# Two transformer blocks on one core: first loads and keys reordered, recurrence products spread over 22 turns

## The chip, the core and the metric

The kernel runs on one core of a Trainium2 chip. A core has a matrix engine (PE, TensorE), a vector engine (DVE), a scalar engine (ACT), a general engine (POOL, GpSimd) and a queue that only issues transfers (SP). Each engine works through its own list of instructions in order and waits on semaphores that other engines raise. The metric is the device time of one execution in microseconds (us), lower is better.

## What is computed

512 tokens of width 1024 pass a first block of two layers and then a second block of one layer. The change touches the first block only: its memory keys and values, its even layer's mixer, and the two MLPs beside which the second block's modulation is summed.

```
mem_n = rmsnorm(mem, mem_norm_gain)                      # 256 memory tokens
for l in range(2):
    h = rmsnorm(x, g[0])
    y = even_mixer(h, ...) if l == 0 else odd_mixer(h, ...)
    x = x + rmsnorm(y, g[1])
    h = rmsnorm(x, g[2])
    kv = mem_n @ w_kv[l]                                 # keys and values
    x = x + rmsnorm(memory_cross_attention(h, mem_n, w_q[l], w_kv[l], w_o[l]), g[3])
    h = rmsnorm(x, g[4])
    x = x + rmsnorm(squared_relu_mlp(h, w_ff1[l], w_ff2[l]), g[5])

# even_mixer: h @ w_in gives u (pooling), q, f (forget gate), i (values), g (output gate), 512 columns each
#   u: mean over 2, 4, 8 and 16 tokens less u, times a 128x128 matrix per group, times a scale
#   q, f, i, g: a gated linear recurrence with 4 heads of 128, normed per head and gated
#   both halves side by side @ w_out
mod = silu(c) @ cond_w + cond_b                          # second block's shifts, scales and gates
```

## The kernel before

**Products.** Every weight matrix comes in chunks of 1 MB into three raw buffers. SP issues the load of chunk r when chunk r - 3 is used up. A chunk has two units. For each unit ACT writes the rounded part (`act_split`, L417) and POOL the rest (`pool_split`, L425); four unit places hold them. PE multiplies three times for each tile (high by high, high by low, low by high, L439 to L441). Who splits how far ahead at which point is written out by hand: `AHEAD` is 3 units.

**Memory stage.** `pe_memory` makes for each layer eight key tiles (one unit each), then four value chunks with two token tiles each. Its first three key tiles run together (`pe_first`). ACT rounds the memory (`act_operand`), makes the root of the mean square (`act_root`, L537 and L540), and rounds x for the even layer. DVE subtracts the low parts (`dve_operand_low`, L556), scales each key tile by the root (L814, event `key_scaled`) and, between key 3 and key 4 of layer 0, makes the low parts and the sum of squares of x (L556, L563). POOL issues the constants and x at the start (L719, L721); then for each key tile c it splits unit c + 3 and issues the write of key c (L797), which waits for `key_scaled` c. Values go the same way (L802, after ACT's L787).

**Even layer.** After the products f, g and q, `pe_even` runs a loop of turns. There are 32 items, four heads by eight levels. At turn n DVE makes the decay difference of item n (L1094), ACT its exponential (L973, L975), POOL the high factor (L1233), DVE the low factor of item n - 2 (L1103), PE the pairs of item n - 4 (L891), and DVE keeps them through a mask (L1172). PE begins with turn 4. In its turns it also has one dense piece each in turns 4 to 11 (i, eight pieces) and 12 to 15 (u, four pieces). A piece stands at the head of PE's turn. The outputs of head h run in the turns of head h + 1 (L930 to L938), with the norm's sum (L520), its root on ACT, and on DVE L1207 to L1216. Pooling group g is made by DVE at turn 18 + 2g (L1146 to L1159), multiplied by PE one turn later (L879), rounded by ACT and subtracted by DVE (L1124) at turn 20 + 2g. After the loop come the outputs of head 3, then the product with w_out.

**MLP.** Up products go in groups of four tiles; group g's down product follows group g + 1's up product. Beside them DVE sums the modulation weights (`dve_mod`, L1389 and L1394) and PE adds over partitions (`pe_mod_sum`, L1415); DVE then adds the bias (`dve_mod_add`, L1407), which waits for PE's sum.

```
        I_FROM, U_FROM = 4, 12
            g = (n - 18 - delay) // 2
            return [g] if (n - delay) % 2 == 0 and 0 <= g < 4 else []
```

## Time and profile before

| | us |
|---|---|
| median of 3 runs | 4018.38 (4016.72 to 4021.52) |
| the profiled execution, its own time | 4018.33 |
| its span, first to last instruction | 4017.0 |
| PE busy | 3639.1 (91%) |
| DVE busy | 2034.4 (51%) |
| ACT busy | 1483.5 (37%) |
| POOL busy | 1529.3 (38%) |
| memory stage, loads included | 0 to 159.1 |
| even layer's f, g and q | 159.1 to 225.7 |
| the loop of turns | 225.7 to 371.8 |

The times of the stages are read from where their instructions stand in the timeline. A row of a timeline gives the start, the duration, the engine, the line, the operation and its tiles, and in brackets how long the engine had been idle before it and what ended that. A row of the windows view gives a stretch, its length, and then the busy time (and count of instructions) of PE, of PE's weight loads (PEld), of DVE, ACT and POOL; behind them stand PE's granted clock (1.00 is 2.4 GHz, 0.5 is 1.2 GHz), the share of the DMA engines in use, and GB/s.

### The profile page before, as it was taken

What the parts mean: (1) busy time and instruction counts of PE and PEld (TensorE: products, weight loads), DVE (VectorE), ACT (ScalarE), POOL (GpSimd) and SP (SyncE); (2) the same over time, 40 slices, a digit from 0 to 9 for tenths busy, and PEclk for the clock granted to TensorE, in tenths of its full rate; (3) what the DMA queues carried; (4) which work ended last, traced back from release to release, by engine and by line L of the source; (5) the groups of instructions that cost most, each with busy time, mean ns of one, the idle gap of its engine ahead of it and who ended that gap; (6) DMA issues with size and microseconds to landing.
All of it is one profiled execution on the core that took longest, in us unless ns stands there. A gap on an engine that the chain in (4) does not pass through costs nothing.

```text
span 4017.0 us, 49459 instructions
## 1 busy us (share of the span) xinstructions
PE 3639.1 (91%) x19310; PEld 2963.9 (74%) x19310; DVE 2034.4 (51%) x3613; ACT 1483.5 (37%) x2332; POOL 1529.3 (38%) x724
## 2 busy tenths in 40 slices
PE   4986889998998889988885889999999999999998
PEld 4875667887766668866774578878978888888885
DVE  2265547556345365234767418998852333323334
ACT  3553433234334342324332423336753223332222
POOL 4741324444323234433220133343344545445452
PEclk8997999999999999999995999999999999999999
DMA  4520214443212133322100123444564444444441
GB/s 158 179 78 13 82 53 139 144 137 110 84 58 74 53 116 127 103 75 76 53 3 22 35 88 114 126 132 178 212 214 138 159 143 155 149 144 156 144 157 53
DMA packets 298038, 445.36 MB, mean 111 GB/s; under 512 B 8144, under 2 KB 219088, under 8 KB 295760
## 3 DMA queue, kind: packets, MB, share of 16 engines
q1 hardware_dynamic: 278640, 371.22, 28.2%
q0 software_dynamic: 19168, 70.98, 5.5%
q8 instruction: 155, 2.54, 0.3%
q14 instruction: 75, 0.61, 0.0%
HBM read 383.45 MB, written 58.72 MB: 110 GB/s over the span
## 4 chain that ended last, share of the span: by engine, by line
PE 74%; DVE 17%; ACT 4%; issue 3%; POOL 1%; DMA 1%; DVEq 0%; POOLq 0%; ACTq 0%; SPq 0%
PE bank L439 21%; PE bank L441 20%; PE bank L440 20%; PE bank L2586 3%; PE bank L520 2%; DVE arena_rw L2111 2%; POOL split_low L425 1%; PE bank L1630 1%; DVE arena L2675 1%; PE bank L1654 1%; DVE arena L2769 1%; DVE arena L2677 1%; DVE arena L2681 1%; PE bank L1288 1%; PE bank L1915 1%
## 5 line engine op out<-in xcount | busy, mean ns | idle before, releaser
L425 POOL TENSOR_TENSOR split_low<-weights,split_high 128x1024 fp32r<-128x1024 f32 x554 | 1387.6, 2511 | 2128.9 <-ACT split_high L417 2128.1
L439 PE MATMUL bank<-normed_high,split_high 128*128 128x512 f32 x2480 | 988.5, 399 | 76.0 <-issue 38.8
L440 PE MATMUL bank<-normed_low,split_high 128*128 128x512 f32 x2480 | 974.6, 393 | 0.0
L441 PE MATMUL bank<-normed_high,split_low 128*128 128x512 f32 x2480 | 973.7, 393 | 0.0
L417 ACT CAST split_high<-weights 128x1024 fp32r<-128x1024 f32 x554 | 574.6, 1048 | 676.1 <-PE bank L441 572.2
L439 PEld LDWEIGHTS bank<-normed_high,split_high 128*128 128x128 f32 x2480 | 471.8, 190 | 185.9 <-issue 52.3
L439 PE MATMUL bank<-hidden_high,split_high 128*128 128x512 f32 x1536 | 600.9, 391 | 7.0 <-ACT hidden_high L2670 4.8
L441 PE MATMUL bank<-hidden_high,split_low 128*128 128x512 f32 x1536 | 599.2, 390 | 0.0
L440 PE MATMUL bank<-hidden_low,split_high 128*128 128x512 f32 x1536 | 599.0, 390 | 0.0
L440 PEld LDWEIGHTS bank<-normed_low,split_high 128*128 128x128 f32 x2480 | 472.2, 190 | 99.1 <-issue 3.1
L441 PEld LDWEIGHTS bank<-normed_high,split_low 128*128 128x128 f32 x2480 | 471.1, 190 | 100.2
L1438 DVE TENSOR_TENSOR branch<-branch,bank 128x512 f32<-128x512 f32 x360 | 243.0, 686 | 510.4 <-PE bank L441 510.2
L439 PEld LDWEIGHTS bank<-hidden_high,split_high 128*128 128x128 f32 x1536 | 289.2, 188 | 68.6 <-ACT hidden_high L2670 5.9
L441 PEld LDWEIGHTS bank<-hidden_high,split_low 128*128 128x128 f32 x1536 | 289.1, 188 | 60.5
L440 PEld LDWEIGHTS bank<-hidden_low,split_high 128*128 128x128 f32 x1536 | 289.3, 188 | 59.8
L2717 DVE TENSOR_TENSOR tmp<-tmp,gates 128x512 f32<-128x512 f32 x56 | 42.4, 757 | 273.1 <-ACT tmp L2657 245.4
L1394 DVE SCALAR_TENSOR_TENSOR tmp<-weights,scalars,tmp 128x256 f32<-128x256 f32 x168 | 155.9, 928 | 5.1
L1491 ACT ACTIVATE arena<-arena 128x512 f32<-128x512 f32 x64 | 40.4, 632 | 263.1 <-DVE arena L1512 263.1
L1512 DVE SCALAR_TENSOR_TENSOR arena<-bank,tmp 128x512 f32<-128x512 f32 x64 | 43.8, 689 | 179.8 <-PE bank L441 171.1
L2527 ACT ACTIVATE branch<-bank 128x512 f32<-128x512 f32 x72 | 43.1, 598 | 239.8 <-PE bank L441 239.8
L2586 PEld LDWEIGHTS bank<-arena 128*128 128x128 f32 x1024 | 120.7, 195 | 7.0 <-issue 5.2
L2586 PE MATMUL bank<-arena 128*128 128x128 f32 x1024 | 121.3, 278 | 4.5 <-DVE arena L2698 3.7
(387 smaller groups left out, 4475.5 us busy)
## 6 DMA issues: line engine op xcount, KB each, us to landing
weights<-in_w_ff SPq DMA_DIRECT2D x64, 1024.0 KB, 5.4
weights<-in_peer_u SPq DMA_DIRECT2D x64, 1024.0 KB, 5.8
weights<-in_peer_v SPq DMA_DIRECT2D x64, 1024.0 KB, 5.1
gate_table<-arena SPq DMA_DIRECT2D x16, 2048.0 KB, 7.4
gates<-gate_table POOLq DMA_DIRECT2D x32, 1024.0 KB, 9.8
weights<-in_cond_w SPq DMA_DIRECT2D x24, 1024.0 KB, 5.2
early_table<-branch SPq DMA_DIRECT2D x72, 256.0 KB, 2.1
lates<-early_table POOLq DMA_DIRECT2D x18, 1024.0 KB, 11.0
```

The lines of the kernel that those rows point to most:

```text
L417: act.do.copy(unit_tiles(u)[0], raw_unit(u)).then_inc(*act.sig("split_high", u))
L425: pool.do.tensor_tensor(lo, raw_unit(u), hi.bitcast(F32), ALU.subtract).then_inc(*pool.sig("split_low", u))
L439: pe.do.matmul(o, ah, bh, start=first, stop=False)
L440: pe.do.matmul(o, ah, bl, start=False, stop=False)
L441: return pe.do.matmul(o, al, bh, start=False, stop=last)
L520: pe.do.matmul(banks.tile("sum", norm)[:, 0:n], matrix, rhs, start=i == 0, stop=i == count - 1).then_inc(*pe.sig("summed", norm, i))
L1394: dve.do.scalar_tensor_tensor(out=total, in0=wt[:, a, :], scalar=g_act[:, CT + a:CT + a + 1], in1=total, op0=ALU.mult, op1=ALU.add).then_i ...
L1438: dve.do.tensor_tensor(y[:, c, :], y[:, c, :], made, ALU.add).then_inc(*dve.sig("y_sum", st, n, c))
L1512: dve.do.scalar_tensor_tensor(out=s, in0=banks.tile("product", (st, "up", g), c), scalar=0.0, in1=root, op0=ALU.max, op1=ALU.mult).then_in ...
L2111: dve.do.scalar_tensor_tensor(out=conv[:, c, :], in0=src, scalar=wc, in1=conv[:, c, :], op0=ALU.mult, op1=ALU.add).then_inc(*dve.sig("conv ...
L2527: act.do.activation(s, banks.tile("product", ("early", g), c), ACT.Gelu).then_inc(*act.sig("gelu", g, c))
L2586: last = pe.do.matmul(bank[:, j * P:(j + 1) * P], hot[:, 0, t, :], hot[:, 1, t, :], start=True, stop=True)
```

## The change

The change does five things.

- **First loads.** POOL issues the load of x only when the memory and the first two key chunks (chunk 0 and 1) have landed. ACT no longer splits four units first: it splits two, then interleaves the next two with the rounding of the memory.
- **Keys.** ACT splits one unit (4) instead of three before the root, and interleaves the rounding of x with the units of the keys. POOL issues the write of key c three splits later (`KEY_LAG`), and the writes of the values likewise. DVE works on x after key 7 instead of after key 3.
- **Modulation sums.** In the second up group of each MLP PE's first three sums stand one product later than before (the first and second) or where they stood (the third).
- **Recurrence.** The second i chunk is loaded and used after u. The pieces stand at turns 4, 6, 8, 10 (i, first chunk), 11, 13, 15, 17 (u), 19, 21, 23, 25 (i, second chunk). Pooling group g is at turn 14 + 2g.
- **Rounding of the mixer's result.** The pooled tiles are first kept in the place of u (`pooled_kept`), since the i products still read the operand. ACT rounds them at turns 29 to 32, the heads 0, 1, 2 at turns 27, 28, 35, and DVE subtracts one turn later. ACT has four instructions more.

```diff
-        for n in "fgqiu":
-            W["E", n] = stream(dram["w_in_ab"], n0="uqfig".index(n) * 512, n_cols=512)
+        W["E", "i"] = []
+        for n, first, n_cols in (("f", 0, 512), ("g", 0, 512), ("q", 0, 512), ("i", 0, 256), ("u", 0, 512), ("i", 256, 256)):
+            ids = stream(dram["w_in_ab"], n0="uqfig".index(n) * 512 + first, n_cols=n_cols)
+            W["E", n] = W["E", "i"] + ids if n == "i" else ids
...
+            pool.wait_ge(at("constants_landed", constant_names[-1]), at("memory_landed"), landed("chunk", 1))
             pool.do.dma_start(x, dram["x"].rearrange("(c p) t -> p c t", p=P)).then_inc(*pool.land("x_landed"))
-            pool.wait_ge(at("constants_landed", constant_names[-1]))
...
-            act_split(AHEAD)
+            first = 2 * W["keys", 0][0]
             for c in range(CT):
+                act_split(first + min(1 + c // 2, FIRST))
                 act_operand("mem", c, mem_raw[:, c, :], mem_gain, mem_hi[:, c, :], mem_square[:, c, :],
                             at("memory_landed"))
-            act_split(2 * W["keys", 0][0] + FIRST + AHEAD)
+            act_split(first + FIRST + 1)
             act_root("mem", 0, NORM_EPS, mem_root, M)
-            for c in range(CT):
-                act_operand(EM, c, x[:, c, :], gain_of(0, 0), h_hi[:, c, :], y[:, c, :], at("x_landed"))
             for l in range(2):
                 for c in range(CT):
                     act_split(2 * W["keys", l][0] + c + AHEAD)
+                    if l == 0:
+                        act_operand(EM, c, x[:, c, :], gain_of(0, 0), h_hi[:, c, :], y[:, c, :], at("x_landed"))
...
                     pool_split(2 * W["keys", l][0] + c + AHEAD)
-                    pool.wait_ge(at("key_scaled", l, c))
-                    pool.do.dma_start(memory_k[l, c], k_out.tile(l, c)).then_inc(*pool.land(*k_written(l, c)))
-                for n, i in enumerate(W["values", l]):
-                    for tk in range(M // P):
-                        pool_split(2 * i + tk + AHEAD - 1)
-                        pool.wait_ge(at("value_scaled", l, n, tk))
-                        pool.do.dma_start(memory_v[l, tk][:, n * 256:(n + 1) * 256], v_out.tile(l, n, tk)
-                                          ).then_inc(*pool.land(*v_written(l, n, tk)))
+                    if c >= KEY_LAG:
+                        pool_key_out(l, c - KEY_LAG)
+                tokens = [(n, tk) for n in range(len(W["values", l])) for tk in range(M // P)]
+                for m, (n, tk) in enumerate(tokens):
+                    pool_split(2 * W["values", l][n] + tk + AHEAD - 1)
+                    if m < KEY_LAG:
+                        pool_key_out(l, CT - KEY_LAG + m)
+                    else:
+                        pool_value_out(l, *tokens[m - KEY_LAG])
+                for n, tk in tokens[-KEY_LAG:]:
+                    pool_value_out(l, n, tk)
+
+        KEY_LAG = 3
+
+        def pool_key_out(l, c):
+            pool.wait_ge(at("key_scaled", l, c))
+            pool.do.dma_start(memory_k[l, c], k_out.tile(l, c)).then_inc(*pool.land(*k_written(l, c)))
+
+        def pool_value_out(l, n, tk):
+            pool.wait_ge(at("value_scaled", l, n, tk))
+            pool.do.dma_start(memory_v[l, tk][:, n * 256:(n + 1) * 256], v_out.tile(l, n, tk)
+                              ).then_inc(*pool.land(*v_written(l, n, tk)))
...
-                    if l == 0 and c == 3:
-                        dve_token_root("mem", 2, 4)
-                        for e in range(CT):
-                            dve_operand_low(EM, e, x[:, e, :], gain_of(0, 0), h_hi[:, e, :], h_lo[:, e, :],
-                                            at("x_landed"))
-                        dve_operand_sum(EM, lambda e: y[:, e, :])
+                if l == 0:
+                    dve_token_root("mem", 2, 4)
+                    for e in range(CT):
+                        dve_operand_low(EM, e, x[:, e, :], gain_of(0, 0), h_hi[:, e, :], h_lo[:, e, :], at("x_landed"))
+                    dve_operand_sum(EM, lambda e: y[:, e, :])
...
-        I_FROM, U_FROM = 4, 12
+        I_TURNS, U_TURNS = (4, 6, 8, 10, 19, 21, 23, 25), (11, 13, 15, 17)
+        PIECE_TURNS = sorted(I_TURNS + U_TURNS)
+
+        UNIT_PIECE = (3, 3, 4, 5, 6, 7, 11, 11)
+        HEAD_FINALS, POOL_FINALS = {27: 0, 28: 1, 35: 2}, {29: 0, 30: 1, 31: 2, 32: 3}
 
         def pool_at(n, delay):
 
-            g = (n - 18 - delay) // 2
+            g = (n - 14 - delay) // 2
             return [g] if (n - delay) % 2 == 0 and 0 <= g < 4 else []
 
         def rec_units(n):
 
-            if n < I_FROM:
-                return 2 * W["E", "i"][0] + AHEAD - 1
-            if n < U_FROM:
-                return 2 * W["E", "i"][(n - I_FROM) // TT] + AHEAD - ((n - I_FROM) % TT == 0)
-            return 2 * W["E", "u"][0] + min(n - U_FROM, 4) + AHEAD
-
+            return 2 * W["E", "i"][0] + 3 - (n < 5) + sum(PIECE_TURNS[j] < n for j in UNIT_PIECE)
...
-                next(i_product if n < U_FROM else u_product, None)
+                if n in PIECE_TURNS:
+                    next(i_product if n in I_TURNS else u_product)
...
-                    banks.give(("pooled", g), ("mixed_low", EM, g))
+                    banks.give(("pooled", g), ("pooled_kept", g))
...
-            pe.wait_ge(empty, at("pairs_kept", hd, N_LV - 1), at("rec_v", 1, 3))
+            pe.wait_ge(empty, at("pairs_kept", hd, N_LV - 1), at("rec_v", hd // 2, 3))
...
-                if I_FROM <= n < U_FROM:
-                    i, tk = (n - I_FROM) // TT, (n - I_FROM) % TT
+                if n in I_TURNS:
+                    i, tk = I_TURNS.index(n) // TT, I_TURNS.index(n) % TT
...
-                    act.wait_ge(at("pooled", g), at("product", (EM, "u"), 3))
-                    act.do.activation(h_hi[:, g, :], banks.tile("pooled", g), ACT.Identity, scale=col("pool_scale", g)
-                                      ).then_inc(*act.sig("mixed_high", EM, g))
+                    act.wait_ge(at("pooled", g))
+                    act.do.activation(upad[:, g, POOL_PAD:], banks.tile("pooled", g), ACT.Identity,
+                                      scale=col("pool_scale", g)).then_inc(*act.sig("pooled_kept", g))
+                if n in HEAD_FINALS:
+                    act_rec_final(HEAD_FINALS[n])
+                if n in POOL_FINALS:
+                    g = POOL_FINALS[n]
+                    act.wait_ge(at("pooled_kept", g), at("product", (EM, "i"), 1, 3))
+                    act.do.copy(h_hi[:, g, :], upad[:, g, POOL_PAD:]).then_inc(*act.sig("mixed_high", EM, g))
...
-            yield
-            act.wait_ge(at("rec_gated", hd), at("product", (EM, "u"), 3))
-            act.do.copy(h_hi[:, 4 + hd, :], s).then_inc(*act.sig("mixed_high", EM, 4 + hd))
+
+        def act_rec_final(hd):
+            act.wait_ge(at("rec_gated", hd), at("product", (EM, "i"), 1, 3))
+            act.do.copy(h_hi[:, 4 + hd, :], e_q[:, hd, :]).then_inc(*act.sig("mixed_high", EM, 4 + hd))
...
-                if 0 <= n - U_FROM < 4:
-                    dve_scaled((EM, "u"), [n - U_FROM], lambda c: upad[:, c, POOL_PAD:])
+                if n in U_TURNS:
+                    dve_scaled((EM, "u"), [U_TURNS.index(n)], lambda c: upad[:, c, POOL_PAD:])
                 for g in pool_at(n, 0):
                     dve_pooling(g)
-                for g in pool_at(n, 2):
+                if n - 1 in HEAD_FINALS:
+                    dve_rec_final(HEAD_FINALS[n - 1])
+                if n - 1 in POOL_FINALS:
+                    g = POOL_FINALS[n - 1]
                     dve.wait_ge(at("mixed_high", EM, g))
-                    dve.do.scalar_tensor_tensor(out=h_lo[:, g, :], in0=banks.tile("pooled", g),
-                                                scalar=col("pool_scale", g), in1=h_hi[:, g, :].bitcast(F32),
-                                                op0=ALU.mult, op1=ALU.subtract).then_inc(*dve.sig("mixed_low", EM, g))
+                    dve.do.tensor_tensor(h_lo[:, g, :], upad[:, g, POOL_PAD:], h_hi[:, g, :].bitcast(F32), ALU.subtract
+                                         ).then_inc(*dve.sig("mixed_low", EM, g))
+            dve_rec_final(2)
             run(dve_rec_output(REC_HEADS - 1))
+            dve_rec_final(REC_HEADS - 1)
...
+        def dve_rec_final(hd):
             dve.wait_ge(at("mixed_high", EM, 4 + hd))
-            dve.do.tensor_tensor(h_lo[:, 4 + hd, :], s, h_hi[:, 4 + hd, :].bitcast(F32), ALU.subtract
+            dve.do.tensor_tensor(h_lo[:, 4 + hd, :], e_q[:, hd, :], h_hi[:, 4 + hd, :].bitcast(F32), ALU.subtract
                                  ).then_inc(*dve.sig("mixed_low", EM, 4 + hd))
...
-                        if g == 1 and c == 0:
-                            mod_sums(0, 1)
-                            mod_sums(0, 3)
-                        mod_sums(g, c)
+                        if g == 1 and c < GROUP - 1:
+                            if c:
+                                mod_sums(c - 1, 5 - 2 * c)
+                        else:
+                            mod_sums(g, c)
```

On POOL, at the start of the key tiles of layer 0 (`memory_k` is the write of a key tile). Before:

```order
13 L425 TENSOR_TENSOR split_low<-weights_78,split_high 128x1024 x2
14 L425 TENSOR_TENSOR split_low<-weights_79,split_high 128x1024 x2
15 L797 DMA memory_k<-arena 128x256
16 L425 TENSOR_TENSOR split_low<-weights_80,split_high 128x1024
17 L797 DMA memory_k<-arena 128x256
18 L425 TENSOR_TENSOR split_low<-weights_80,split_high 128x1024
```

After:

```order
13 L427 TENSOR_TENSOR split_low<-weights_78,split_high 128x1024 x2
14 L427 TENSOR_TENSOR split_low<-weights_79,split_high 128x1024 x2
15 L427 TENSOR_TENSOR split_low<-weights_80,split_high 128x1024 x2
16 L427 TENSOR_TENSOR split_low<-weights_78,split_high 128x1024
17 L816 DMA memory_k<-arena 128x256
18 L427 TENSOR_TENSOR split_low<-weights_78,split_high 128x1024
```

The first write of a key stood behind four splits and stands behind seven.

On DVE, in the memory stage (L814 before and L832 after scale the keys, L556 and L563, then L558 and L565, work on x). Before:

```order
4 L814 TENSOR_TENSOR arena<-bank,arena 128x256 x4
5 L581 COPY token_root<-bank 128x2
6 L556 SCALAR_TENSOR_TENSOR normed_low<-residual,columns,normed_high 128x512 x8
7 L563 TENSOR_TENSOR branch<-branch 128x512 x7
8 L814 TENSOR_TENSOR arena<-bank,arena 128x256 x12
```

After:

```order
4 L832 TENSOR_TENSOR arena<-bank,arena 128x256 x8
5 L583 COPY token_root<-bank 128x2
6 L558 SCALAR_TENSOR_TENSOR normed_low<-residual,columns,normed_high 128x512 x8
7 L565 TENSOR_TENSOR branch<-branch 128x512 x7
8 L832 TENSOR_TENSOR arena<-bank,arena 128x256 x8
```

The 15 instructions on x moved behind four more keys.

On PE, in the loop, at the first pooled product (L879 before, L897 after; L891 and L909 are pairs, L439 to L441 and L441 to L443 a dense piece, here of u). Before:

```order
1372 L891 MATMUL bank<-branch 128x128 x8
1373 L520 MATMUL bank<-tmp_60,arena 128x512
1374 L891 MATMUL bank<-branch 128x128 x4
1375 L879 MATMUL bank<-tmp_62,branch 128x512
1376 L891 MATMUL bank<-branch 128x128 x4
1377 L891 MATMUL bank<-arena 128x128 x4
```

After:

```order
1245 L441 MATMUL bank<-normed_high,split_high 128x512
1246 L442 MATMUL bank<-normed_low,split_high 128x512
1247 L443 MATMUL bank<-normed_high,split_low 128x512
1248 L897 MATMUL bank<-tmp_62,branch 128x512
1249 L909 MATMUL bank<-branch 128x128 x4
1250 L948 MATMUL bank<-arena 128x128
1251 L951 MATMUL bank<-arena 128x128
```

A dense piece now stands ahead of the pooled product, where only pairs stood.

## Rows read from the trace of the kernel before

**Rows 1.** Windows, memory stage and loop: stretch, length, then busy us by engine

```profile
39.37:45.81 6.44, 0.00 (x1) 0.03 (x1) 1.42 (x4) 6.40 (x12) 3.08 (x3) 0.88 0.06 20
60.19:77.65 17.46, 0.00 (x1) 0.03 (x1) 11.55 (x20) 0.00 (x0) 5.90 (x5) 0.63 0.05 16
77.65:159.07 81.42, 73.04 (x579) 71.59 (x579) 3.40 (x8) 29.63 (x39) 69.49 (x49) 0.97 0.59 196
225.73:286.40 60.67, 59.08 (x415) 55.06 (x414) 39.96 (x55) 33.49 (x52) 32.15 (x22) 1.00 0.22 70
286.40:371.80 85.40, 44.69 (x226) 36.67 (x225) 60.77 (x114) 38.51 (x59) 14.82 (x16) 0.76 0.04 13
```

**Rows 2.** Timeline of POOL in the memory stage

```profile
4.64 0.90 POOL L721 DMA_DIRECT2D residual<-in_x  x1
16.55 9.48 POOL L425 TENSOR_TENSOR split_low<-weights,split_high 128x1024 fp32r<-128x1024 f32 x4 [11.00 <-ACT split_high L417]
42.70 0.58 POOL L797 DMA_DIRECT2D memory_k<-arena  x1 [16.67 <-DVE arena L814]
...
71.71 0.56 POOL L797 DMA_DIRECT2D memory_k<-arena  x1 [17.30 <-DVE arena L814]
...
98.50 2.37 POOL L425 TENSOR_TENSOR split_low<-weights,split_high 128x1024 fp32r<-128x1024 f32 x1 [0.17 <-ACT split_high L417]
```

**Rows 3.** Timeline of ACT in the memory stage

```profile
11.46 0.21 ACT L1378 ACTIVATE scalars<-columns 128x8 f32<-128x8 f32 x1
15.35 1.99 ACT L417 CAST split_high<-weights 128x1024 fp32r<-128x1024 f32 x2 [3.68 <-DMA weights<-in_w_mem_kv]
...
41.46 0.42 ACT L540 ACTIVATE arena<-arena 128x256 f32<-128x256 f32 x1
...
50.84 1.99 ACT L417 CAST split_high<-weights 128x1024 fp32r<-128x1024 f32 x2
```

**Rows 4.** DMA queues from 10 to 15 us: packets, MB, share of 16 engines

```profile
q0 software_dynamic: 370, 1.52, 81.1%
q1 hardware_dynamic: 387, 0.38, 23.5%
```

**Rows 5.** Timeline of DVE: x in the memory stage, then a modulation step in MLP 0

```profile
60.31 5.39 DVE L556 SCALAR_TENSOR_TENSOR normed_low<-residual,columns,normed_high 128x512 fp32r<-128x512 f32 x8
...
625.82 2.51 DVE L1394 SCALAR_TENSOR_TENSOR tmp<-weights,scalars,tmp 128x256 f32<-128x256 f32 x1
628.25 0.15 DVE L1407 SCALAR_TENSOR_TENSOR modulation<-bank,columns 128x2 f32<-128x2 f32 x1
```

**Rows 6.** Windows of single turns: one with an i piece, one with u, two bare

```profile
242.12:245.89 3.77, 3.77 (x35) 3.77 (x33) 2.73 (x4) 3.05 (x5) 2.75 (x4) 1.00 0.76 241
270.36:277.42 7.06, 7.06 (x40) 6.07 (x39) 5.09 (x6) 2.74 (x5) 3.55 (x2) 1.00 0.10 31
286.20:288.15 1.95, 1.95 (x18) 1.76 (x16) 1.95 (x3) 0.00 (x0) 1.95 (x3) 1.00 0.00 0
```

**Rows 7.** Waits in loop and tail (225.73 to 394.41): total, times, longest

```profile
DVE arena L1172 <- PE bank L891: 29.2, 15, 4.0
...
PE bank L879 <- DVE tmp L1159: 23.1, 4, 6.6
```

**Rows 8.** Groups by line in the loop: count, busy us, mean ns, idle before

```profile
L1094 DVE TENSOR_TENSOR branch<-arena 128x512 f32<-128x512 f32 x28 | 24.3, 876 | 0.0
L1172 DVE COPY_PREDICATED arena<-arena,bank 128x512 f32<-128x512 uint32 x28 | 20.5, 732 | 29.2 <-PE bank L891 29.2
...
L1147 DVE TENSOR_TENSOR arena<-arena 128x527 f32<-128x527 f32 (+3 forms) x10 | 7.0, 697 | 0.0
```

**Rows 9.** Timeline of PE in MLP 0, second up group

```profile
618.87 0.98 PE L1415 MATMUL bank<-const_mean,tmp 128*128 128x1 f32 x4 [5.23 <-DVE tmp L1394]
...
621.52 0.77 PE L439 MATMUL bank<-normed_high,split_high 128*128 128x512 f32 x1 [1.67 <-POOL split_low L425]
```

**Rows 10.** Timeline of ACT at the same place

```profile
617.91 1.04 ACT L417 CAST split_high<-weights 128x1024 fp32r<-128x1024 f32 x1
```

3 lines of the change are left out of this document (2 added, 1 removed).

## The prediction

> **What bounds the kernel now.** I read the windows by stage first, to see where PE idles, then the timelines of POOL, ACT and DVE in those stretches, to see who comes last. The change touches three places.
>
> *Memory stage.* PE does nothing for 6.44 us from 39.37 and for 17.46 us from 60.19 [rows 1]. Both times POOL is the one it lacks, and POOL in turn waited 16.67 and 17.30 us at the write of a key for DVE's scaling of that key [rows 2]: first because the root ends at 41.88 [rows 3], then because DVE works on x from 60.31 [rows 5], 11.55 us busy in the stretch [rows 1]. Splits that PE needs are queued behind these two writes on POOL. From 77.65 on PE is busy 73.04 of 81.42 us [rows 1]: there the split is held by ACT's half of it (0.17 us of wait on ACT at 98.50 [rows 2]), which follows ACT's scaling of a value tile.
>
> *Loop of turns.* Up to 286.4 PE is busy 59.08 of 60.67 us; afterwards 44.69 of 85.40, while DVE is busy 60.77 and the granted clock is 0.76 [rows 1]. All dense pieces lie in the first part. In the second, PE waits 23.1 us for DVE's pooling before four products and DVE waits for pairs, 29.2 us over the loop [rows 7]. Each waits for the other, in turn.
>
> *MLP.* PE waits 5.23 us for the modulation sum and then 1.67 us for a split [rows 9].
>
> The rest of the kernel is not touched.
>
> **First loads.** Between 10 and 15 us the queue with x moved 1.52 MB and the one with the keys 0.38 MB [rows 4]; chunk 0 landed at about 15.3 [rows 3]. So at 10 us some 0.4 MB of it were missing; at the 0.38 MB per us of both queues together it lands at about 11.1 and chunk 1 at 13.9. But POOL waits for chunk 1 before it issues x (0.90 us [rows 2]), and its splits are queued behind that: they start at 14.8 instead of 16.55. ACT, free at 11.67 [rows 3], is in time. The gain is 1.8 us where chunk 0 alone would give 3.7. PE's three first tiles go on from the third split, so from about 22.1 instead of 24.0. A few of its products have run before that, so I put the root, now done at 41.88 [rows 3], at 39.6. Bounds: 0 to 4 us earlier.
>
> **Keys and x.** Split 4 follows the first three tiles directly (ACT 34.2, POOL 36.6 by 2.37 us each [rows 2]), so key 4 starts as the sum ends, and the 6.44 us are gone. What is late next is split 5: ACT does the root and two of the eight x steps first (8.96 us for eight from 41.88 to 50.84 [rows 3], 2.2 for two), so 41.8, split 42.9, POOL 45.3. PE idles about 5.3 us there. Then POOL paces: splits of 2.37 with a write of 0.58 [rows 2] give 47.7, 50.6, 53.6 and 56.5 for units 6 to 9, and the values of layer 0 start at 56.5 instead of 77.65: 21.1 us. DVE's 11 us on x now run beside the values, and x is wanted at the end of the stage: nothing.
>
> Small terms behind that. The first value product ran partly at the low clock (0.97 in the stretch [rows 1], so up to 2.4 us of 81.42): minus 1.8. `token_root` is now copied after key 7, whose buffer waits for the write of key 3, three splits back: one value split is late by 0.9. Value tile m needs the buffer of m - 4, whose write is issued one step later than its own split: 0 to 2 us, I take 1. The sum of the stage is 21.1 + 1.8 - 0.9 - 1 - 0.5 = **20.5 us** gained, bounds 13 and 25.
>
> DVE on x and POOL now run at the same time, which the trace has elsewhere: an instruction of DVE with two SBUF inputs took 2.51 us at 625.82 where a split ran [rows 5]. The Trainium skill ("SBUF — State Buffer", section "SBUF: two separate sides") says that such a DVE instruction and a GpSimd one that reads SBUF lock each other out for a whole instruction, whichever starts first. By it the 15 instructions could hold up eight splits by up to 0.7 us each, 5 us on this path instead of the 0.5 above; with DVE off the path it costs nothing there.
>
> **The loop.** The cost of a turn on PE: 3.77 us with an i piece, 7.06 with u (outputs in it), 0.97 bare [rows 6]. On DVE the decay difference takes 0.88 and the masked copy 0.73 [rows 8]; with the low factor (0.6, my estimate between these and its half width) that is 2.2 per turn, waits for POOL's port included. A step of pooling is 0.70 [rows 8], so group g takes about 0.7 (g + 1) + 1.8. I walk the new turns in four parts.
> - Turns 4 to 10: PE 4 x 3.77 + 3 x 0.97 = 18.0. DVE has 7 x 2.2 = 15.4, head 0's keys 2.5 and 5 of backlog: 23. DVE bounds.
> - Turns 11 to 18: PE 4 x 7.06 + 4 x 0.97 + 2 pooled products of 1 = 34. DVE 17.6, keys and outputs 6, pooling 0 and 1 5.7: 29. PE bounds, and its u pieces cover pooling 0 and 1, which in the old order covered nothing: that is where the wait of 23.1 [rows 7] shrinks.
> - Turns 19 to 27: DVE 9 x 2.2 + keys and outputs 7 + pooling 2 and 3 8.5 less overlap = 33; an i piece of 2.8 doesn't cover 3.9 and 4.6, so DVE also waits twice for a pooled product and pairs (2 each) and once for a root: 38.
> - Turns 28 to 35: the same work as before, some 21 from turn 28's start to its last pair, plus six roundings moved here (0.6 each), less two waits of 0.7 for ACT: 24.
>
> Together 119, with 2 for stretches at the low clock 121, against 145 now. The loop gains **24 us**. Its bounds: DVE was busy 39.96 + 60.77 = 100.7 us in it [rows 1], so no more than 45; and 0, if every turn waits as in the second part now. Kept for the range: 8 and 36. ACT's four extra copies (0.6 each) lie beside DVE in turns 28 to 32. The splits of the second i chunk and of w_out come one to eight turns before their use. The tail after the loop (outputs of head 3, first tiles of w_out) stays, since it hangs on head 3.
>
> **Modulation sums.** I cost this edit at a small loss. The sum's wait of 5.23 us [rows 9] covers another one: the next product needs a split whose ACT half began at 617.91 [rows 10], after DVE's chain, with no link to the sum. PE would wait until 621.52 anyway. The sum (0.5 us at full clock) leaves an idle stretch for a busy one, and DVE's bias step at 628.25 [rows 5] now waits for it about 0.9 us, with the next `relu` queued behind it. **Plus 1 us** for both MLPs; bounds 0 and 3.
>
> **Sum.** 4018.33 (the profiled execution; the median of the runs, 4018.38, is the same) - 20.5 - 24 + 1 = 3974.8, so 3975.
>
> **Rivals.**
> 1. *PE stays at the low clock in turns 19 to 35.* It has 34 us of work there at full clock (4 x 2.8 + 17 x 0.97 + 6) with waits between. At 0.76 it was busy 44.69 in the second part now [rows 1]. If half of the turns run at the low level, 16 us come back, and the loop gains 8: 3991. Against it: the u pieces now fill the middle. Chance 0.15. The Trainium skill ("TensorE: Matmul & The Clock Gate", section "HAM oscillation — how this bites in real kernels") says that a PE that waits between bursts falls back to half rate again and again; by that rule, this case.
> 2. *The loop reaches DVE's own time,* 101 to 105 us, since waits vanish with balance: 3956. For it: DVE had idle time only where it waited for PE. Against: pooling still stands between two pairs. Chance 0.1.
> 3. *The modulation sums bring their wait,* 5.2 us in each MLP, because the split comes sooner than I read: 3964. Against: [rows 9, 10]. Chance 0.06.
> 4. *Port.* The memory stage gains 13 because splits and DVE lock each other out: 3982. Chance 0.1.
> 5. *Slower.* A piece at the head of a turn holds the pairs back, DVE waits for them, and the next turn's output waits for DVE, so that PE and DVE never overlap. Then the loop takes PE's 84 us (32 x 0.97 + 8 x 2.8 + 4 x 5.7 + 8) plus DVE's 100.7 = 185 instead of 146: 4018 - 20 + 39 + 1 = 4038. It decides from a loop of 166 us on. Against it: up to 286.4 PE was busy 59.08 and DVE 39.96 us of 60.67 [rows 1], which is overlap. Chance 0.04.
> 6. *The change doesn't do what it says:* x's load or the key writes turn out to wait longer than they did (chunk 1 late, a full ring of four key buffers), and both gains stay under 4 us: about 4012. Chance 0.02.
>
> **Numbers.** The forecast has 0.53. Its own bounds are 4018 - 25 - 36 + 0 = 3957 and 4018 - 13 - 8 + 3 = 4000, which takes in rivals 1, 3, 4 and nearly 2. A measurement of this kernel tells 0.2%, 8 us, from no change. Faster 0.94, same 0.02, slower 0.04.
>
> **What would show it.** Memory stage: POOL's first split at 14.8; one idle of about 5 us before key 5; values from about 56; the stage's end (first f product) near 138.5. Loop: some 120 us long, PE's wait before the pooled products under 12 us, DVE over 80% busy in it. MLP: the wait before the second product of the group grows to about 7.9 us and ends on the split. Wrong would be a wait on a key write that reappears, a loop over 137 us, or a wait at the sum's new place.

## The result and the profile after

The changed kernel takes 3989.55 us (median of 4 runs, 3986.77 to 3990.26) against 4017.72 us for the kernel before (4 runs, 4016.72 to 4021.52): the ratio is 0.993, with a 95% interval of 0.9918 to 0.9942. It is faster, by 28.2 us; 43.5 us were forecast. Profiled execution against profiled execution, the gain is 4018.33 - 3986.77 = 31.6 us. By the places where PE starts its stages, 18.7 us of it come before the first f product (now at 140.41, 159.07 before), 12.4 us in the loop up to the first product of `w_out` (133.64 us long instead of 146.08), and 0.5 us in the two MLP groups. f, g and q between them take 66.66 us in both.

The windows of the changed kernel, which answer to [rows 1] (stretch, length, then busy us and instructions of PE, PEld, DVE, ACT and POOL, the granted clock, DMA share, GB/s): the gap before key 5, the values of layer 0, from there to the first f product, and the loop in two parts.

```profile
38.91:44.06 5.15, 0.01 (x1) 0.03 (x1) 0.90 (x3) 5.15 (x8) 2.50 (x2) 0.95 0.00 0
55.18:87.98 32.80, 26.44 (x192) 25.92 (x193) 19.45 (x18) 9.77 (x14) 22.59 (x17) 0.90 0.49 165
87.98:140.41 52.43, 47.67 (x389) 46.56 (x387) 3.40 (x8) 19.77 (x25) 46.67 (x33) 1.00 0.61 201
207.07:268.47 61.40, 55.88 (x348) 48.98 (x347) 47.83 (x75) 33.26 (x52) 28.03 (x21) 0.97 0.16 52
268.47:340.71 72.24, 45.75 (x293) 40.12 (x292) 54.95 (x93) 40.29 (x64) 21.57 (x16) 0.83 0.09 30
```

The two idle stretches of [rows 1], 6.44 and 17.46 us, have become one of 5.15. But the values of layer 0, PE from 77.65 to 106.85 in the kernel before, now take longer:

```profile
77.65:106.85 29.20, 25.61 (x193) 25.09 (x193) 0.00 (x0) 9.86 (x14) 22.43 (x17) 0.93 0.56 185
```

The same work takes 32.80 instead of 29.20 us. Why, the timelines of the changed kernel tell: DVE (scaling of the keys 4 to 7, then the root of the tokens), then ACT (scaling of value tiles), each with the idle time ahead of it and what ended it.

```profile
38.39 1.42 DVE L832 TENSOR_TENSOR arena<-bank,arena 128x256 f32<-128x256 f32 x4 [7.37 <-ACT arena L542]
49.65 0.42 DVE L832 TENSOR_TENSOR arena<-bank,arena 128x256 f32<-128x256 f32 x1 [9.84 <-DMA memory_k<-arena]
...
59.91 0.42 DVE L832 TENSOR_TENSOR arena<-bank,arena 128x256 f32<-128x256 f32 x1 [4.27 <-DMA memory_k<-arena]
60.25 0.15 DVE L583 COPY token_root<-bank 128x2 f32<-128x2 f32 x1
60.32 9.72 DVE L558 SCALAR_TENSOR_TENSOR normed_low<-residual,columns,normed_high 128x512 fp32r<-128x512 f32 x8
```

```profile
60.49 0.48 ACT L790 ACTIVATE arena<-bank,token_root 128x256 f32<-128x256 f32 x1 [6.88 <-DVE token_root L583]
...
78.17 0.47 ACT L790 ACTIVATE arena<-bank,token_root 128x256 f32<-128x256 f32 x1 [3.33 <-DMA memory_v<-arena]
```

Keys go through four buffers. Key 7 needs the one of key 3, whose write POOL now issues three splits after its turn and which has to land; so it is scaled at 59.91, the root of the tokens is copied behind it, and ACT, which scales the values by it, stands idle for 6.88 us with the next split queued behind. PE waits 3.57 us for that split and then starts at the low level (granted clock 0.90 in the stretch). Some of these 6.88 us ACT would have waited anyway, for PE's first product of values (run `lag1` below tells how many). Value tiles meet the same ring: 15.6 us of waits of ACT on `memory_v`, six of them.

The waits in the loop and the tail (207.07 to 363.2), total, times, longest, against [rows 7]:

```profile
DVE arena L1202 <- PE bank L909: 21.9, 12, 4.7
...
PE bank L897 <- DVE tmp L1189: 12.4, 2, 7.0
```

DVE's waits for pairs went from 29.2 to 21.9 us, PE's for the pooled product from 23.1 (four times) to 12.4 (twice). The two left are groups 2 and 3. PE, DVE and POOL at group 2:

```profile
278.43 2.08 PE L897 MATMUL bank<-tmp,branch 128*128 128x512 f32 x2 [7.04 <-DVE tmp L1189]
280.29 1.92 PE L909 MATMUL bank<-branch 128*128 128x128 f32 x8
```

```profile
272.70 2.34 DVE L1176 COPY arena<-arena 128x2 f32<-128x2 f32 x1
...
278.89 0.42 DVE L1129 TENSOR_TENSOR branch<-arena,branch 128x256 f32<-128x256 f32 x1
282.25 0.73 DVE L1202 COPY_PREDICATED arena<-arena,bank 128x512 f32<-128x512 uint32 x1 [2.94 <-PE bank L909]
```

```profile
272.68 2.34 POOL L427 TENSOR_TENSOR split_low<-weights,split_high 128x1024 fp32r<-128x1024 f32 x1 [5.77 <-ACT split_high L419]
...
314.18 5.24 POOL L427 TENSOR_TENSOR split_low<-weights,split_high 128x1024 fp32r<-128x1024 f32 x2 [6.12 <-ACT split_high L419]
```

Two things stand here. PE waits 7.04 us for the mean of the group with the pair of the same turn queued behind it, and DVE then waits 2.94 us for that pair. And DVE's copy of two columns takes 2.34 us, exactly as long as POOL's split beside it; its like took 0.17. The same happens in part at DVE's turn 28 (the splits stand in POOL's turn 26), where the second of these POOL rows covers two splits:

```profile
314.98 2.23 DVE L1120 TENSOR_TENSOR branch<-arena 128x512 f32<-128x512 f32 x1
317.13 2.57 DVE L1129 TENSOR_TENSOR branch<-arena,branch 128x256 f32<-128x256 f32 x1
```

Their like took 0.68 and 0.42.

In MLP 0 PE's wait is now in one piece, and the sum comes behind the second product ([rows 9] has 5.23 and 1.67):

```profile
590.23 0.77 PE L441 MATMUL bank<-normed_high,split_high 128*128 128x512 f32 x1 [7.87 <-POOL split_low L427]
...
597.12 0.50 PE L1447 MATMUL bank<-const_mean,tmp 128*128 128x1 f32 x4
```

A word on the measure. In all twelve kernels below, the part behind the loop, from the first product of `w_out` to the last of PE, is nearly the same code, and in the profiled executions it took between 3627 and 3636 us. At one place in it, a group of eight products took 3.67 us in the changed kernel (from 461.07, granted clock 1.00 around it) and 5.37 in `lag1` (from 458.82, granted clock 0.84). So single times carry some 5 us that say nothing of an edit, and small effects are read below from where PE's stages start.

### The profile page after: what moved, and what is told of

It reads as the page before. It is cut to its first block, busy times and chain, and to the rows that moved or that the text cites. A ratio compares the mean times of both kernels' runs of the same rounds, so it can differ in the third digit from the quotient of the medians.

```text
span 3985.5 us, 49467 instructions
## 1 busy us (share of the span) xinstructions
PE 3638.2 (91%) x19310; PEld 2962.6 (74%) x19310; DVE 2050.4 (51%) x3613; ACT 1484.3 (37%) x2336; POOL 1529.6 (38%) x724
## 4 chain that ended last, share of the span: by engine, by line
PE 73%; DVE 16%; ACT 4%; issue 3%; POOL 2%; DMA 1%; DVEq 0%; POOLq 0%; ACTq 0%; SPq 0%
PE bank L441 21%; PE bank L443 20%; PE bank L442 20%; PE bank L2619 3%; PE bank L522 2%; DVE arena_rw L2144 2%; POOL split_low L427 2%; DVE arena L2708 1%; PE bank L1663 1%; DVE arena L2802 1%; DVE arena L2710 1%; DVE arena L2714 1%; PE bank L1687 1%; PE bank L1320 1%; PE bank L1948 1%
## 5 line engine op out<-in xcount | busy, mean ns | idle before, releaser
L441 PE MATMUL bank<-normed_high,split_high 128*128 128x512 f32 x2480 | 991.3, 400 | 88.5 <-issue 38.8
L443 PE MATMUL bank<-normed_high,split_low 128*128 128x512 f32 x2480 | 976.1, 394 | 0.0
L441 PEld LDWEIGHTS bank<-normed_high,split_high 128*128 128x128 f32 x2480 | 473.3, 191 | 200.0 <-issue 65.9
L441 PE MATMUL bank<-hidden_high,split_high 128*128 128x512 f32 x1536 | 601.0, 391 | 6.9 <-ACT hidden_high L2703 4.7
L443 PE MATMUL bank<-hidden_high,split_low 128*128 128x512 f32 x1536 | 599.2, 390 | 0.0
L443 PEld LDWEIGHTS bank<-normed_high,split_low 128*128 128x128 f32 x2480 | 472.2, 190 | 100.7
L441 PEld LDWEIGHTS bank<-hidden_high,split_high 128*128 128x128 f32 x1536 | 289.2, 188 | 68.5 <-ACT hidden_high L2703 5.8
L443 PEld LDWEIGHTS bank<-hidden_high,split_low 128*128 128x128 f32 x1536 | 289.2, 188 | 60.5
L2750 DVE TENSOR_TENSOR tmp<-tmp,gates 128x512 f32<-128x512 f32 x56 | 42.4, 756 | 272.9 <-ACT tmp L2690 245.5
```

The lines of the kernel that those rows point to most:

```text
L441: pe.do.matmul(o, ah, bh, start=first, stop=False)
L443: return pe.do.matmul(o, al, bh, start=False, stop=last)
```

## The experiments

**Each part alone.** `mem_only` is the kernel before with the memory stage of the change and nothing else; `loop_only` has the new chunk order and the new loop alone.

```
mem_only:  pool_inputs, act_memory, pool_memory (KEY_LAG 3), dve_memory of the change
loop_only: SHARED, W["E"], I_TURNS, U_TURNS, UNIT_PIECE, pool_at, the finals of the change
```

> The kernel before with the memory stage alone changed (x issued behind chunk 1, splits and key writes in the new order, x behind the keys of layer 0); loop and modulation sums as before. Account A (additive: each part of the change gives what its stage gave in the changed kernel, where the first f product starts 18.7 us earlier): the stage brings 18.7 us, so about 4018.4 - 18.7 = 3999.7, within 2. Rival B (the memory stage's gain is partly paid back in the loop by transfers or splits that meet it earlier, and the loop's shortfall is that debt): the stage again starts f 18.7 us earlier, but the time falls by 10 us or less, 4008 and more.

> The kernel before with the recurrence loop alone changed (chunk order f, g, q, i1, u, i2, pieces over 22 turns, pooling two to four turns earlier, roundings behind it). Account A (additive; the loop is short of its 24 us by its own waits and has nothing to do with the memory stage): 12 us, so about 4006. The forecast's own number for this part was 24 us, 3994. Rival B (interaction with the memory stage): the loop alone brings 20 us or more, 3998 or less.

`mem_only` took 4004.17 us (4000.52 to 4013.33) against 4017.11 for the kernel before on the same chip, ratio 0.9974, interval 0.9961 to 0.9986. `loop_only` took 4005.25 (4001.59 to 4015.95), ratio 0.9977, 0.9966 to 0.9989. Here are the windows of the two loops, `mem_only` first:

```profile
206.51:352.25 145.74, 104.31 (x639) 92.03 (x638) 99.61 (x168) 72.07 (x111) 47.96 (x37) 0.84 0.11 37
```

```profile
226.04:358.42 132.38, 101.24 (x640) 89.41 (x638) 102.09 (x168) 73.49 (x115) 49.97 (x37) 0.88 0.12 40
```

In `mem_only` f starts at 139.85, 19.2 us earlier than in the kernel before, and its loop is as long as before. In `loop_only` the loop is 13.7 us shorter. Together that is 32.9 us, where the change has 18.7 + 12.4 = 31.1: the parts add, and the loop's shortfall is no debt of the memory stage. By the medians they are 12.9 and 11.9 us, 24.8 together where the change has 28.2. `loop_only` is where its account A had it (4006); the median of `mem_only` is 4.5 us above what was expected. The part behind its loop was 1.8 us longer than before in the profiled execution; for the other executions nothing shows where it went.

**Modulation sums back in their old place,** in the changed kernel:

```
-                        if g == 1 and c < GROUP - 1:
-                            if c:
-                                mod_sums(c - 1, 5 - 2 * c)
-                        else:
-                            mod_sums(g, c)
+                        if g == 1 and c == 0:
+                            mod_sums(0, 1)
+                            mod_sums(0, 3)
+                        mod_sums(g, c)
```

> The changed kernel with the modulation sums back in their old place. Account A (the sum's wait only covered the wait for the split): the same time as the changed kernel within 2 us, 3987 to 3992, and in the trace the second up product starts as long behind the first one as in the kernel before. Rival C (moving the sums brought their waits of 5.2 us each, and the loop gained less): 10 us slower than the changed kernel, 3999.

3988.60 us (3980.52 to 3993.18), ratio 0.9924, interval 0.9908 to 0.9941. The wait is in two pieces again, and the second up product starts at 589.94, 7.89 us behind the first one's end; in the changed kernel it is 7.87.

```profile
587.28 0.98 PE L1447 MATMUL bank<-const_mean,tmp 128*128 128x1 f32 x4 [5.24 <-DVE tmp L1426]
589.94 0.77 PE L441 MATMUL bank<-normed_high,split_high 128*128 128x512 f32 x1 [1.67 <-POOL split_low L427]
```

From the end of the first up product to the down products of the group before it is 27.91 and 28.24 us in the changed kernel (MLP 0 and 1), 28.97 and 29.00 with the sums in their old place. That is 1.8 us less in all with the sums moved. But the kernel before, with the same old order, took 27.31 and 29.37 us, 1.3 us less in all than `sums_undone`, so most of the 1.8 can be chance. In the time nothing is seen, and the wait of 5.2 us was never to be had.

**Writes one split behind instead of three.**

```
-        KEY_LAG = 3
+        KEY_LAG = 1
```

> The changed kernel with the writes of keys and values one split behind instead of three (KEY_LAG 1). Account A (in the changed kernel the writes come so late that the ring of four buffers is full: DVE waits up to 4.3 us for a key's write to land, so the root of the tokens comes at 60.3, and ACT waits 2.2 to 3.3 us for value writes; the value stage of layer 0 takes 32.8 us instead of 29.2): the waits on landed writes go, values of layer 0 take 29 us, f starts 3.5 to 4.5 us earlier, 3985 to 3986. Rival D (the value stage is longer because DVE's work on x and POOL's splits share a port): the splits stay as long and late, no gain, 3989.5. Rival E (with the writes earlier POOL waits for the scaling of keys again, as before the change): values of layer 0 start 2 us or more later than 55.2, and the kernel is slower than 3990.

3988.90 us (3980.61 to 3991.63), ratio 0.993, interval 0.9914 to 0.9947: by the time alone this cannot be told from the changed kernel. By the trace it can. Windows of the values of layer 0 and of the rest up to f, then DVE's last key and ACT's first value:

```profile
55.80:84.01 28.21, 23.78 (x193) 23.26 (x193) 25.10 (x15) 9.87 (x14) 23.47 (x17) 1.00 0.58 192
84.01:136.18 52.17, 47.44 (x388) 46.50 (x387) 3.40 (x8) 19.77 (x25) 46.77 (x33) 1.00 0.61 202
```

```profile
54.39 0.42 DVE L832 TENSOR_TENSOR arena<-bank,arena 128x256 f32<-128x256 f32 x1 [2.45 <-PE bank L443]
54.73 0.15 DVE L583 COPY token_root<-bank 128x2 f32<-128x2 f32 x1
```

```profile
58.95 0.47 ACT L790 ACTIVATE arena<-bank,token_root 128x256 f32<-128x256 f32 x1 [5.25 <-PE bank L443]
```

From key 5 on no wait on a write is left (key 4 still waits 1.37 us for one); keys and values wait for PE's products alone. ACT's first value waits for PE until 58.95, 3.2 us after the values start; in the changed kernel it came 5.3 us after that, so the late token root cost ACT some 2 us. The values take 28.21 us instead of 32.80, at full clock, and f starts at 136.18, 4.2 us earlier. Rival D falls with it: DVE's 15 steps on x take even longer beside the splits (26.8 us, 19.3 in the changed kernel, 10.85 in the kernel before), and hold up little. PE's three waits for splits within the values are 4.4 us, 3.6 in the kernel before, where no DVE step stood beside them: 0.8 us. Rival E falls too, since the values start at 55.80.

**ACT's half of split 5 ahead of the root.**

```
-            act_split(first + FIRST + 1)
+            act_split(first + FIRST + 2)
             act_root("mem", 0, NORM_EPS, mem_root, M)
```

> The changed kernel with ACT's half of split 5 ahead of the root of the memory instead of behind it and two x steps. In the changed kernel it began at 40.46 and PE stood 5.15 us ahead of key 5. Account A (PE waits for the split alone, and POOL paces the keys from then on): ACT's half at 33.2, POOL's at 38.0, the wait before key 5 goes, the root comes up to 0.5 us later; values of layer 0 start at 51 to 52 instead of 55.2, f 3 to 4 us earlier. Rival F (writes: a key's scaling needs a free buffer and the writes are issued by POOL behind these splits): keys 4 to 7 are scaled as late as now, token root at 60 as now, so ACT waits for it still and f starts within 1 us of 140.4.

One run, 3989.58. The wait before key 5 is gone, but PE waits 3.40 us before key 6: ACT now does three x steps at once before the next split, at 42.54.

```profile
42.02 0.62 ACT L554 ACTIVATE branch<-residual 128x512 f32<-128x512 f32 x1
42.54 1.03 ACT L419 CAST split_high<-weights 128x1024 fp32r<-128x1024 f32 x1
```

The values start at 54.89 instead of the 51 to 52 of account A, and f at 139.49, 0.9 us earlier: the outcome of rival F. The write ring (the token root came at 59.3, the waits on `memory_k` stayed) is a part of it, and the wait that moved one key on is the other, which neither account had.

**The pair ahead of the pooled product.** In PE's turn, the pooled product goes behind the pair and the output:

```
-                for g in pool_at(n, 1):
-                    ...
                 bank, empty = banks.take("pairs", hd, lv)
                 ...
                 next(outputs, None)
                 next(turns, None)
+                for g in pool_at(n, 1):
+                    ...
```

> The changed kernel with PE's pooled product queued behind the pair (and the output) of its turn instead of ahead of them. In the changed kernel PE waits 7.04 and 5.39 us for the means of groups 2 and 3 with the next pair queued behind, and DVE then waits 2.94 and 2.93 us for that pair (1.19 and 1.17 at groups 0 and 1). Account L (the loop is short of its gain because DVE and PE take turns at the pooled products): DVE's waits for these pairs go, the loop takes 128 us instead of 133.6. Rival C (it is the low clock in turns 19 to 35: the same matmuls at half the rate): PE's waits move elsewhere, the loop stays within 2 us of 133.6. Rival P (the port between DVE and the splits that the change moved into turns where DVE sets the pace): also within 2 us.

One run, 3982.15. The loop takes 130.23 us. DVE's waits for pairs fall from 21.9 to 16.4, the 5.5 us that were expected; but DVE is 3.2 us longer busy (105.99 instead of 102.77), and the loop gets 3.4. The same loop in `best1` (below) takes 126.66. So the edit is worth 3.4 to 7 us, against the 5.6 of account L (128); here is the second part of the loop in the two kernels:

```profile
267.89:336.72 68.83, 49.11 (x302) 43.60 (x300) 57.26 (x93) 39.86 (x63) 19.09 (x16) 0.80 0.09 31
```

```profile
262.69:327.95 65.26, 45.01 (x299) 40.83 (x299) 55.77 (x93) 39.77 (x63) 21.84 (x16) 0.84 0.10 33
```

The 3.6 us between them come in three pieces. 1.2 us come before the pooled product of group 3, where the pair at the start of this part took PE 1.91 us at the low level in `pair_first`, so that DVE kept it 1.4 us later. 0.8 us come at the last root, whose product took 2.07 us in `pair_first` and 1.13 in `best1`. The other 1.6 us (9.58 against 7.99 us from one output's product to the root's) lie between, where POOL's last three multiplications stand beside DVE's steps. In the changed kernel, as in `best1`, POOL's are long and DVE's as long as ever:

```profile
325.52 2.53 POOL L1265 TENSOR_TENSOR branch<-arena,branch 128x256 f32<-128x256 f32 x1 [3.76 <-ACT branch L993]
328.53 1.93 POOL L1265 TENSOR_TENSOR branch<-arena,branch 128x256 f32<-128x256 f32 x1 [0.48 <-ACT branch L993]
```

In `pair_first` POOL's are short, and DVE's three steps beside them take 1.22, 1.21 and 0.94 us, 0.5 each more than their like:

```profile
319.41 0.99 POOL L1265 TENSOR_TENSOR branch<-arena,branch 128x256 f32<-128x256 f32 x1 [3.76 <-ACT branch L993]
322.95 0.99 POOL L1265 TENSOR_TENSOR branch<-arena,branch 128x256 f32<-128x256 f32 x1 [2.55 <-ACT branch L993]
```

`split5` and `warm` fell as `pair_first` did, the other kernels with the new loop (`loop_only`, `sums_undone`, `lag1`, `thin`, `pair_thin`, `pair_thin_warm`, `best1`, `best2`) as the changed kernel. These are the times that two engines would show that shut each other out of a port, POOL waiting in the one case and DVE in the other. The code of that place is the same, and nothing here shows what decides it. With these 1.6 us taken off, the pair's edit is worth 5.0 us.

**Three thin splits.** POOL splits one eighth of units 9, 10 and 11 of the loop (those at 272.7 and 314.2); the other seven eighths of the low part of these weights are left out:

```
+                few = slice(0, 1 if u - 2 * W["E", "i"][0] in (9, 10, 11) else chunks[u // 2].n_k)
-                pool.do.tensor_tensor(lo, raw_unit(u), hi.bitcast(F32), ALU.subtract
+                pool.do.tensor_tensor(lo[:, few], raw_unit(u)[:, few], hi.bitcast(F32)[:, few], ALU.subtract
```

> The changed kernel in which POOL splits only 128 of 1024 columns of three units of weights: those whose splits ran at 272.7 and 314.2 to 319.4, where DVE sets the pace (most of the low half of these weights is left out of the computation; ACT's halves and all products stay). Rival P (port: DVE's instructions beside these splits took 2.2 + 0.5 and 1.6 + 2.2 + 1.0 us longer than their like): the excess goes, the loop takes 127 to 129 us instead of 133.6. Account L (turn taking at the pooled products) and rival C (clock): DVE's time there is covered by waits anyway, the loop takes 132 to 134.

One run, 3991.50. The loop takes 130.38 us, 3.3 less, and DVE's busy time in it falls from 102.77 to 96.66, all of it in the second part:

```profile
269.46:338.44 68.98, 49.56 (x293) 44.45 (x292) 48.87 (x93) 40.17 (x64) 15.93 (x16) 0.80 0.10 31
```

The port is real and was worth 6.1 us of DVE; a little over half of that reaches the loop's length, because DVE waits 2.8 us more: 1.7 for ACT's exponentials of a head (L1207 here), 0.5 for pairs, 0.6 for an output. The expectation of rival P was 127 to 129 us, that of the others 132 to 134; the measured 130.4 lies between. Both edits together:

> Both loop edits together: the pooled product behind the pair, and three POOL splits cut to 128 of 1024 columns (most of the low half of these weights left out). Alone they made the loop 130.2 and 130.4 us long instead of 133.6. If turn taking and port are two causes that add: 133.6 - 3.4 - 3.3 = 127, within 1. If both only free the same wait: 130. If together they release more than alone, since either cause hid the other: 124 or less.

One run, 3980.72. The loop takes 123.41 us, 10.2 less than in the changed kernel, and 121 had been forecast for it:

```profile
267.64:329.65 62.01, 46.53 (x302) 41.22 (x301) 49.16 (x93) 40.30 (x64) 16.64 (x16) 0.88 0.10 34
```

Against 127 for simple addition and 124 for causes that cover each other, this is the second. But with the pair's edit at 5.0 us simple addition gives 125.3, and the 1.9 us that remain are no more than the low level moved this loop between `pair_first` and `best1` (1.2 + 0.8). That the causes cover each other is not shown.

**Is it the clock?** Idle products of 128x512 fill PE's waits ahead of two pooled products (12 each, then 18) and of two heads' outputs (8 each, then 12), in banks that the true product overwrites; first in the changed kernel, then on top of both edits. The lines for the pooled products:

```
+                    for _ in range(12 if g >= 2 else 0):
+                        pe.do.matmul(bank, h_hi[:, 0, 0:P], h_hi[:, 0, :], start=True, stop=True)
                     pe.wait_ge(at("pool_mean", g), at("pool_w_landed"))
```

> The changed kernel with 12 idle products of 128x512 on PE ahead of the pooled products 2 and 3, and 8 ahead of the outputs of heads 2 and 3, in banks that the true product then overwrites: PE is busy where it waited. Rival C (clock): the products and pairs behind the waits run at full clock (1.1 + 1.1 us instead of 2.1 + 1.9), DVE's waits of 2.9 us shrink by 1.8 each, the loop takes 127 to 130 us instead of 133.6. Account L: the waits are for DVE and not for PE's rate, the loop stays within 1.5 us of 133.6; more than 135 if the idle products themselves come to stand in the way.

> The kernel with both loop edits, and on top 18 idle products of 128x512 ahead of pooled products 2 and 3 and 12 ahead of the outputs of heads 2 and 3, so that PE is busy in its waits. With the causes of turn taking and port taken away, what the low clock is worth by itself: rival C (clock) says that the granted clock of the last 72 us, 0.84, goes to 0.95 or more and the loop loses another 4 to 6 us, some 122. The account without the clock says that it stays within 1.5 us of the kernel with both edits, about 127, whatever the granted clock is.

One run each, 3991.94 and 3975.73. The loops take 133.61 and 122.58 us. The second part in both:

```profile
267.50:339.71 72.21, 54.09 (x334) 47.15 (x332) 56.65 (x93) 40.30 (x64) 18.79 (x16) 0.88 0.09 30
```

```profile
268.47:329.65 61.18, 53.49 (x359) 47.56 (x359) 49.31 (x93) 39.79 (x63) 16.20 (x16) 0.97 0.11 35
```

In `warm` the length stayed, but not because the clock did nothing. In the second part it rose from 0.83 to 0.88. At group 2 the idle products ended 4.35 us before the mean, and the product behind was still at the low level, 2.08 us. At group 3 they ended 1.99 us before it, and there the product took 1.12 us and the pair 1.05; in the changed kernel they took 2.07 and 1.91. Here is that product, `warm` first:

```profile
291.13 1.12 PE L900 MATMUL bank<-tmp,branch 128*128 128x512 f32 x2 [1.99 <-DVE tmp L1195]
```

```profile
292.06 2.07 PE L897 MATMUL bank<-tmp,branch 128*128 128x512 f32 x2 [5.39 <-DVE tmp L1189]
```

From that pair to the last three multiplications of POOL the loop of `warm` is 1.9 us ahead of the changed kernel's. There it falls the other way, DVE's steps take 1.22, 1.21 and 0.95 us, and 1.6 us are lost again. So account L came out by its number, in part by luck. In `pair_thin_warm`, where these multiplications go as in `pair_thin`, the clock is 0.97 instead of 0.88 and the second part 0.8 us shorter. The low level of these turns follows from PE's waits. It costs 0.8 us where both edits are in, 1.9 at group 3 of the changed kernel, and at its group 2, where the idle products came too early, it was not tested. That is well under the 8 us of rival 1, which came out near the measured time by the wrong road.

**A version from the findings.** `best1` is the changed kernel with KEY_LAG 1, split 5 ahead of the root, splits of the keys two ahead of the x steps, and the pair ahead of the pooled product. `best2` mends what its trace showed:

```
best1:  KEY_LAG = 1;  act_split(2 * W["keys", l][0] + c + AHEAD + (2 if l == 0 else 0))
best2:  KEY_LAG = 2;  act_split(2 * W["keys", l][0] + (min(c + AHEAD + 2, 11) if l == 0 else c + AHEAD))
        UNIT_PIECE = (3, 3, 4, 5, 6, 7, 11), unit 11 by ACT at turn 33; and behind POOL's loop:
+            pool.wait_ge(at("mixed_low", EM, 3))
+            pool_split(rec_units(N_TURNS))
```

> The changed kernel with the edits that the runs so far point to: writes one split behind (KEY_LAG 1), ACT's half of split 5 ahead of the root, ACT's splits of the keys two further ahead of its x steps, and the pooled product behind the pair. Expected: the wait before key 5 gone and no new one over 1.5 us before key 6, values of layer 0 from 50 instead of 55.2 and 28.2 us long instead of 32.8, f from 130 to 131.5 instead of 140.4, loop 130.2 instead of 133.6, modulation as in the changed kernel: 13 us faster than the changed kernel, 3975 to 3978. If POOL paces the keys whatever ACT does (a split of 2.4 and a write of 0.58 each from 38.9 on), values start at 52 or later and 3 us of this are missing.

`best1`: 3980.49 us (3977.43 to 3985.62), ratio 0.9909, interval 0.9892 to 0.9926. f starts at 134.63 instead of the 130 to 131.5 that were expected. The time is 2.5 us above the 3975 to 3978 that were expected. With one split of lag, the write of key 0 stands ahead of split 5, and POOL waits there for DVE's scaling of that key, which follows the root (from 38.51; the row below names PE as the releaser, the code waits for DVE); PE still idles 3.31 us before key 5:

```profile
39.23 0.57 POOL L816 DMA_DIRECT2D memory_k<-arena  x1 [3.48 <-PE bank L443]
39.82 2.37 POOL L427 TENSOR_TENSOR split_low<-weights,split_high 128x1024 fp32r<-128x1024 f32 x1
```

> The kernel best1 with three repairs: writes two splits behind (KEY_LAG 2) so that POOL does split 5 before it waits for key 0; ACT's splits run ahead of its x steps only up to unit 11, so that none waits 5.15 us for PE in front of the value scaling; and the last split of the loop (unit 11) taken by POOL after DVE's last rounding, when DVE waits for the last pairs, instead of at turn 27. Expected if these three waits were what best1 lacked: the 3.31 us before key 5 go, values of layer 0 from 50 instead of 54, f at 130 to 131 instead of 134.6; DVE's step of 2.57 us beside that split back to 0.4, the loop 1 to 3 us shorter than in best1 and in the kernel with the pair ahead alone (126.7 and 130.2: 124 to 128); in all 3973 to 3976. If DVE's later writes take up the port time wherever they stand, the loop stays at 127 to 130 and the time at 3977 to 3980. If the later split holds up the fourth tile of w_out in the tail, the loss shows there: more than 3.6 us of wait ahead of it.

`best2`: **3967.43 us** (3966.41 to 3970.86), ratio 0.9873, interval 0.9857 to 0.9889: 50.6 us faster than the kernel before on the same chip and 22 under the changed kernel's median. POOL does splits 4 and 5 in one go and then writes; f starts at 132.25, 8.2 us earlier than in the changed kernel (the values at 52.19, not 50: PE waits 1.19 us at key 6 and 2.35 at the first value). The loop takes 125.15 us, 8.5 less. The two stages give 16.7 us together, and profiled execution against profiled execution the gain is 15.9; so of the 22 us between the medians some 5 are not explained, nor is it shown why the time is below the 3973 to 3976 that were expected. DVE still waits 10.7 us for the landings of key writes (four times, 4.2 at most), but the token root comes at 52.64, before ACT needs it. The split moved behind POOL's loop lies in DVE's wait for the last pairs:

```profile
33.70 4.76 POOL L427 TENSOR_TENSOR split_low<-weights,split_high 128x1024 fp32r<-128x1024 f32 x2 [8.58 <-ACT split_high L419]
39.59 0.57 POOL L816 DMA_DIRECT2D memory_k<-arena  x1 [1.13 <-PE bank L443]
...
318.15 2.34 POOL L427 TENSOR_TENSOR split_low<-weights,split_high 128x1024 fp32r<-128x1024 f32 x1 [2.85 <-DVE normed_low L1153]
```

```profile
300.07 2.24 DVE L1120 TENSOR_TENSOR branch<-arena 128x512 f32<-128x512 f32 x1
302.23 1.07 DVE L1129 TENSOR_TENSOR branch<-arena,branch 128x256 f32<-128x256 f32 x1
...
320.41 0.73 DVE L1202 COPY_PREDICATED arena<-arena,bank 128x512 f32<-128x512 uint32 x1 [2.34 <-PE bank L903]
```

DVE's step that took 2.57 us beside the second split takes 1.07 (POOL's next multiplication is still beside it), and the wait ahead of the fourth tile of `w_out` is 3.61 us, as in the changed kernel.

## Why the prediction was right in its direction and too large by half

Faster was right, and the time lies in the range (3957 to 4000), 15 us above the forecast. Of the three terms, one held, one fell short by 2 us and one by half.

*First loads: near in sum.* Chunk 1 landed at 14.37 (13.9 in the estimate), but POOL's first split began at 15.95 instead of 14.8, a gain of 0.6 us and not 1.8. The root ended at 38.29, 1.3 us earlier than put, by a road that was not in the sum: with the rounding of the memory between ACT's splits, DVE's low parts begin at 14.15 instead of 22.14, and PE, whose first product waited for them until 24.01, begins at 18.46. The sum is near by two errors that go opposite ways, which is luck.

*Keys and x: right to the value stage.* The idle stretch before key 5 is 5.15 us (5.3 forecast), it ends on the split, and the values start at 55.18 (56.5). That is 22.5 us gained where 21.1 were summed.

*Small terms: the step that failed in this stage.* The sum took 2.4 us for the late token root, the ring of value buffers and the port, and gave 1.8 for the clock, 0.6 net. The stage of values lost 3.6 us, of which `lag1` gives back more than all (28.21 us). The prediction had both mechanisms, the buffer that waits for the write of three splits back and the value buffer of m - 4, and priced them by the issue of the write alone. What was left out is its landing: in the changed kernel the writes took a median of 3.7 us (keys) and 4.1 (values) from issue to landing, and that of key 3, issued at 54.96, released DVE at 59.91.

```profile
memory_k<-arena POOLq DMA_DIRECT2D x8, 128.0 KB, 3.7
memory_v<-arena POOLq DMA_DIRECT2D x8, 128.0 KB, 4.1
```

So the token root came at 60.25, 5.5 us later than in `lag1` (54.73), and ACT's first value some 2 us late, not 0.9. PE waited 3.57 us for the split behind it where it waits 1.44 in `lag1`, and the products that follow took 8.66 us at the low level instead of 5.98. These 2.1 and 2.7 us make up the difference between the two kernels' values (32.80 and 28.21), and the gift of 1.8 for a full clock turned into its opposite. The Trainium skill ("DMA: Bandwidth & Descriptors", section "Anatomy of one DMA — SWDGE (gpsimd) path") states a fixed 2.0 us and a part by size, for 128 KB some 2.3 us as an estimate; the measured ones are 1.4 to 1.8 us longer, with 1 MB loads of weights on the way beside them. Either number, counted into the ring, would have shown a wait. "A wait on a key write that reappears" stood among the signs of being wrong, and it is what was seen.

*Port in the memory stage (rival 4): wrong.* DVE's fifteen steps on x took 19.3 us beside the splits instead of 11, but the splits beside them took 2.4 to 2.7 us, and `lag1`, with the same 15 steps beside its splits, has the values in 28.21 us: the port costs PE some 0.8 us there, where this rival took 7.5 off the gain.

*The loop: 12.4 us of 24.* By the prediction's four parts, the forecast was 23, 34, 38 and 24, with 2 for the clock. Measured were 23.0 (to 230.1), 38.4 (to 268.5), 42.4 (to 310.9) and 29.8 (to 340.7). The mechanism was right: the u pieces cover pooling 0 and 1, PE's wait for pooled products fell to 12.4 us (under 12 forecast), and DVE was 77% busy (over 80 forecast, a sign that was missed). Two sums are off in the prediction's own terms: the loop before was 146.1 us and not 145, and part four adds up to 23.2 and not 24. Three terms were too small. Part two: 2.8 us of waits on state and means, and a root's and a transpose's products, which the count of PE's work left out. Part three: two waits of DVE of 2 us each were put in for the pooled product; they were 2.9 each, and the copy beside the split took 2.2 more. Part four: the price of 2.2 us for a turn on DVE came from a mean in which the port's waits lay where PE set the pace; the change puts two splits of `w_out` (POOL's turn 26) beside DVE's turn 28, where DVE does, and DVE's two steps beside them took 3.7 us more than their like. That a moved piece moves its split too, and past whom, was asked of the memory stage and not of the loop. `pair_first`, `thin` and both together (130.2, 130.4, 123.4 us) show what the two causes cost: together 10.2 us, all of it in parts three and four, which fall from 72.2 to 62.0, the 62 that were put for them. But 4 of these 10.2 us are waits for the pooled product that the forecast had counted. Of the shortfall of 12.6 us the traces place 5.9 at the port (2.2 + 3.7) and 1.8 at the pooled products; the 4.4 of part two no experiment took back, and the rest isn't traced.

*Low clock (rival 1): there, but small.* At a granted clock of 0.97 instead of 0.88 in the second part the loop was 0.8 us shorter, and full rate at group 3 alone gave 1.9 in `warm`; the rival had 8. The rule of the Trainium skill that the prediction set beside this rival ("TensorE: Matmul & The Clock Gate", section "HAM oscillation — how this bites in real kernels") describes what the trace shows, a PE that falls back between bursts (granted clock 0.83).

*DVE's own time (rival 2): not reached.* The loop takes 133.6 us where 101 to 105 were this rival's.

*Modulation sums: right.* The wait grew to 7.87 us (7.9 forecast) and ends on the split. From first up product to down products the two MLPs took 0.5 us less than before in all (56.15 against 56.68), where a loss of 1 was put; the same code moved by 1.3 there, so neither sign is shown. Rival 3 is refuted by `sums_undone`. Rivals 5 and 6 didn't occur.

## What to carry to other kernels

A write that is queued later holds its buffer from the computation to the landing, so a ring must cover the lag in steps plus the landing; here two splits of lag instead of three, with the same four buffers, took away ACT's wait on the token root and kept the queue free for the splits. The waits of DVE on landings that were left (10.7 us) cost nothing, since nobody waited for DVE there. When work is moved between stretches that different engines bound, move in thought everything that it drags along: the splits of POOL that cost next to nothing beside PE's long products cost DVE up to their full length beside DVE's chain (2.2 of 2.34 us, 3.7 of 5.24). In a queue that runs in order, put what the other engine waits for (the pair) ahead of what itself waits (the pooled product).

## What the runs showed of the hardware

A copy on DVE of 128x2 elements within SBUF took 2.34 us beside a split of POOL that took 2.34 us, from 272.70 and 272.68, and its like 0.17. It has one SBUF input. The Trainium skill ("SBUF — State Buffer", section "SBUF: two separate sides") names fp32 copies within SBUF beside instructions with two SBUF inputs as holders of the shared port, and the trace agrees: the short one waits for the whole of the long one. In the loop of `loop_only` DVE's instructions summed to 113.6 us, 20.5 more than if each had taken the shortest time of its line and shape there: about a fifth, an upper bound for what the port cost. In the kernel before it was 18.0 of 111.3.

Who gets the port first changes who pays, and the same code went both ways. At the last three multiplications of the loop POOL took 2.53, 1.93 and 1.08 us in the changed kernel, and DVE's steps their usual time; in `pair_first` POOL took 0.99, 0.99 and 0.73 and DVE's three steps 0.5 us each more. The loop, which hung on DVE there, was 1.6 us longer for it.

The same loop code took 130.23 us in one kernel and 126.66 in another, with granted clocks of 0.80 and 0.84 in its second part: 1.6 us are the port and 2.0 products at the low level. Why PE was at the low level at these places in one kernel and not in the other, no run shows. It sets a bound of some 3 us on what a single trace can say of such a loop.
